# The query and key units of the first mixer take their accumulators from five PSUM banks in fixed pairs, instead of from a rotation of three and a side pair

## What is computed

```python
u = rmsnorm(x, g_mix)
q, k, v, z, xbc, dt, g_a, g_s = split(u @ w_in)      # weights of 2048 rows
q, k = apply_rope(q), apply_rope(k)                  # 16 query heads, 4 key heads of 64
attn = sliding_window_sink_attention(q, k, v, sinks)
y = ssd_chunked(silu(conv4(xbc)), dt, ...)           # gated by z, normed
h = x + (sigmoid(g_a) * (attn @ w_attn_br) + sigmoid(g_s) * (y @ w_ssd_br)) @ w_o
h = h + (silu(f @ w_gate) * (f @ w_up)) @ w_down     # f = rmsnorm(h)
h = h + sigmoid(rmsnorm(h) @ w_ple_gate) * (p @ w_ple_proj)
x = rmsnorm(h)                                       # and then the second block:
q, kv, gates, conv_in = split(rms_norm(x) @ w_in_2)  # attention, a 31-tap convolution,
...                                                  # an output projection and a gated FFN
```

## Time and profile before

| | us |
|---|---|
| median of 3 runs (2759.24 to 2760.5) | 2760.45 |
| the profiled execution, its own time | 2762.22 |
| its span | 2760.4 |
| TensorE busy | 2713.8 (98%) |
| VectorE busy | 1961.4 (71%) |
| ScalarE busy | 1416.7 (51%) |
| GpSimd busy | 101.0 (4%) |
| DMA engines, mean busy share of q1 (weights) | 56.7% |

### The profile page before, as it was taken

How to read it: one execution, slowest core, us unless ns; L and a number is a source line. 1 busy time by engine, 2 the same in 40 slices (tenths; PEclk the granted TensorE clock), 3 DMA queues, 4 the chain that set the end, 5 groups by cost and what they waited for, 6 DMA issues and landing times.

```text
span 2760.4 us, 41660 instructions
## 1 busy us (share of the span) xinstructions
PE 2713.8 (98%) x16606; PEld 2383.3 (86%) x16606; DVE 1961.4 (71%) x2940; ACT 1416.7 (51%) x2102; POOL 101.0 (4%) x189
## 2 busy tenths in 40 slices
PE   8999999999999999999999999999999999999998
PEld 7788888888888888888888899988888888888887
DVE  7568777757677776677666778876788775677765
ACT  6455555544455554455445551256655553455543
POOL 1320000000000000000000000000000000000000
PEclk9999999999999999999999999999999999999999
DMA  7466556555568888877656566863355556555554
GB/s 240 135 197 227 176 180 194 184 187 193 197 225 287 279 282 297 294 275 276 208 186 204 185 194 229 277 236 98 133 179 200 187 190 192 181 191 192 183 195 141
DMA packets 166610, 573.19 MB, mean 208 GB/s; under 512 B 19872, under 2 KB 26736, under 8 KB 165904
## 3 DMA queue, kind: packets, MB, share of 16 engines
q1 hardware_dynamic: 151216, 521.86, 56.7%
q0 software_dynamic: 15056, 48.65, 4.9%
q10 hardware_dynamic: 144, 0.01, 0.0%
HBM read 530.86 MB, written 38.90 MB: 206 GB/s over the span
## 4 chain that ended last, share of the span: by engine, by line
PE 90%; DVE 6%; ACT 2%; DMA 1%; issue 1%; POOL 0%; DVEq 0%; SPq 0%; ACTq 0%; POOLq 0%
PE PS L950 89%; DVE wl L1914 1%; DVE CC L1922 1%; DMA raw<-in_w_in 1%; ACT wh L1371 1%; PE PS L1286 0%; DVE SQA L1914 0%; DMA XC<-KTC 0%; DVE QT L1914 0%; DVE Z L1914 0%; DVE H L1914 0%; ACT SX1b L1371 0%; DVE TC L1922 0%; DVE RB L1973 0%; DVE CC L1914 0%
## 5 line engine op out<-in xcount | busy, mean ns | idle before, releaser
L1914 DVE TENSOR_TENSOR wl<-raw,wh 128x1024 fp32r<-128x1024 f32 (+3 forms) x892 | 1044.2, 1195 | 464.5 <-ACT wh L1371 462.6
L1371 ACT ACTIVATE wh<-raw 128x1024 fp32r<-128x1024 f32 (+3 forms) x892 | 898.0, 1031 | 522.1 <-PE PS L950 416.0
L950 PE MATMUL PS<-CHt,wh 128*128 128x512 f32 x2816 | 886.1, 396 | 1.9 <-DVE wl L1914 1.9
L950 PE MATMUL PS<-BIGt,wh 128*128 128x512 f32 (+1 forms) x2816 | 757.4, 357 | 2.9 <-DVE TA L1914 1.2
L950 PE MATMUL PS<-AHt,wh 128*128 128x512 f32 (+1 forms) x2080 | 636.9, 386 | 14.1 <-DVE wl L1914 11.1
L950 PEld LDWEIGHTS PS<-CHt,wl 128*128 128x128 f32 x2816 | 529.0, 188 | 124.8
L950 PE MATMUL PS<-CHt,wl 128*128 128x256 f32 x2816 | 553.5, 278 | 0.0
L950 PEld LDWEIGHTS PS<-BIGt,wl 128*128 128x128 f32 x2304 | 436.0, 189 | 79.1 <-issue 0.2
L950 PE MATMUL PS<-BIGt,wl 128*128 128x256 f32 x2304 | 498.9, 279 | 0.0
L950 PEld LDWEIGHTS PS<-BIGt,wh 128*128 128x128 f32 x2816 | 436.1, 191 | 7.7 <-issue 4.9
L950 PEld LDWEIGHTS PS<-AHt,wl 128*128 128x128 f32 x1952 | 368.7, 189 | 80.0 <-issue 0.7
(11 more groups left out here) (307 smaller groups left out, 1633.5 us busy)
## 6 DMA issues: line engine op xcount, KB each, us to landing
raw<-in_w_up SPq DMA_DIRECT2D x264, 512.0 KB, 4.8
raw<-in_w_in SPq DMA_DIRECT2D x200, 512.0 KB, 4.2
raw<-in_w_down SPq DMA_DIRECT2D x132, 512.0 KB, 4.3
raw<-in_w_gate SPq DMA_DIRECT2D x88, 512.0 KB, 5.5
raw<-in_w_down SPq DMA_DIRECT2D x56, 384.0 KB, 3.6
raw<-in_w_ssd_br SPq DMA_DIRECT2D x32, 512.0 KB, 4.4
raw<-in_w_o SPq DMA_DIRECT2D x32, 512.0 KB, 4.3
PKR<-in_w_in SPq DMA_DIRECT2D x32, 512.0 KB, 5.3
```

The costliest lines, as they stand in the source:

```text
L950: return e.matmul(o, l, r, start=start, stop=stop, skip_group_check=True)
L1371: return e.activation(o, x, f, **k)
L1914: return e.tensor_tensor(o, x, y, op)
```

## The change

The four query units and the key unit get fixed pairs: `ev_q` 0: 0, 1; `ev_q` 1: 3, 4; `ev_q` 2: 2, 0; `ev_q` 3: 1, 3; `ev_k`: 4, 2. All five are now set aside, that is, they no longer move the counter `gb`. `bank_free` is changed so that a query or key unit waits for the last holder of bank 3 or 4 like for any other bank, and the first later unit that takes bank 3 or 4 waits for the scan (`ssd_d`) as before. The number and order of sub-steps and of all steps in the plan stay as they are.

```diff
-            banks=(3, 4) if i == 1 else (0, 1, 2),
+            banks=((0, 1), (3, 4), (2, 0), (1, 3))[i],
...
-    add("w_in", 0, 16, 1024, "U1", "ev_k", 0, mode="turn", gens2=[stage("full_u1", 0, 4)], gens=[("rope_k", 0, [0, None, 1, 2, None])])
+    add("w_in", 0, 16, 1024, "U1", "ev_k", 0, mode="turn", banks=(4, 2), gens2=[stage("full_u1", 0, 4)], gens=[("rope_k", 0, [0, None, 1, 2, None])])
...
-        aside = u.banks == (3, 4)
+        aside = u.ev in ("ev_q", "ev_k")
...
-            if prev is None or units[prev].ev == "ev_q" and b in (3, 4):
-                if prev is not None or b in (3, 4) and units[n].ev != "ev_q":
-                    e.wait_ge(ssd_d.sem, ssd_d.at(3, "xd1"))
+            ahead = ("ev_q", "ev_k")
+            if b in (3, 4) and units[n].ev not in ahead and (prev is None or units[prev].ev in ahead):
+                e.wait_ge(ssd_d.sem, ssd_d.at(3, "xd1"))
+                return
+            if prev is None:
                 return
             emptied(prev)
```

## The result

The changed kernel takes 2771.82 us (median of 6 runs, 2769.33 to 2775.31), against 2760.97 for the kernel before (6 runs, 2759.24 to 2764.48). The ratio is 1.0039, with a 95% interval of 1.0029 to 1.0049: slower by 10.9 us. The forecast was 2765.1 with a range up to 2769.0, so the time lies above the range. The profiled execution is the longest of the six (own time 2775.31, span 2773.5).

A forecast was written before the change was run, and what follows sets the result against it. TensorE, busy for 98% of the span, was taken to bound the kernel. The terms -5.0 - 1.7 + 8.8 + 2.6 = +4.7 us, on a median of 2760.45, gave 2765.1 us, range 2760.5 to 2769.

The forecast's parts named there:

- Step 1, the waits of TensorE: Query and key units: `ev_v` starts without its 3.2 us wait, at full clock (2.96 us), and ends 6.6 us earlier.
- Step 1, the keys: First scores: `KDU` lands at 87.3, TensorE idles 1.6 us without loss of clock, and 5.0 us is gained.
- The second rival: First scores: keys come later, TensorE stands 2.5 us or more and the clock falls; 2768.5 us, chance 0.12.
- Step 2: At `ev_z` 4: the 1.74 us wait goes, since the new holder was joined a unit earlier; 1.7 us gained.
- Step 3: Second mixer's start: `ev_ca` 0 waits for `ev_pg` 7's bank, net 8.8 us lost, plus 2.6 us for the clock.
- Steps 4 and 5: Joints at `ev_q2` 0 and `ev_h` 24: nothing lost at the first, 0 to 0.1 us at the second.
- the queue behind `ev_ca` 0: Second mixer: splits queued on ScalarE behind that wait have enough cover; counted as nothing, up to 1 us.

The follow-up runs named there:

- `keep_count`: The changed kernel with its new pairs, but the counter `gb` still moved by 8 in the five units as before: 2761.37 us, ratio 1.0002.
- `mixer_order`: The changed kernel with the second mixer's rotation written (1, 2, 0) for (2, 0, 1): 2759.12 us, ratio 0.9993.
- `hold_both`: The changed kernel with load 29 held until `RO<-KT` has landed and load 30 until `KDU` has: 2765.08 us, ratio 1.0015.
- `both_fixes`: The changed kernel with the second mixer's rotation (1, 2, 0) and loads 29 and 30 both held: 2755.24 us, ratio 0.9979.
- `after_again`: The changed kernel itself, unaltered, timed and profiled a second time: 2770.65 us, ratio 1.0032.
- `first_only`: The changed kernel with the second mixer's rotation (1, 2, 0) and only load 29 held: 2754.9 us, ratio 0.9975.

## Why the prediction was wrong

- **Step 1, the waits of TensorE: right.** 0.80 us for the `wl` of the key unit (0.8 predicted), no wait and a full clock at `ev_v`, arrival at the scores at 85.85 (85.7). The 2.96 us for the clock at `ev_v` came from a single execution, though. In `keep_count` the wait there was 3.68 us and the low clock lasted only from 73.55 to 76.8, of which half, 1.6 us, is lost.
- **Step 1, the keys: the step that failed.** It said "weight loads that now start sooner share the DMA engines, for which I take 0.2". They cost 2.1 us on `RO<-KT` in the first profile (82.25 against 80.14 for the rotation behind it) and 1.0 to 1.3 us in the other three with early loads, and in the first profile 2.7 us more on `KDU`. And it said "I count no loss of clock here", from a case with 1.74 us of idle time. For the wait that it forecast this held: behind 1.37 and 1.42 us the clock stayed at 1.00. But the wait had become 2.55 to 6.14 us, and the clock fell behind each of them. The gain of step 1 came out at 1.95 - 1.7 = 0.25 us (`mixer_order`, less the 1.7 us of `ev_z` 4; 2.5 us either way by the interval of that run) instead of 5.0. The base of the sum was sound: with the loads held the scores began at 87.31 for 87.3, and steps 1 and 2 together gave -5.8 for -6.7.
- **The second rival is what happened**, and I had it at 0.12. It gave 2768.5 because the keys' delay was counted as 0.9 us and the clock as 2.4. The whole collision costs 3.9 us in `mixer_order`, and 5.0 to 6.8 between the changed kernel and `hold_both` (+10.85 and +9.05, less the +4.0 of `hold_both`).
- **Step 2: right.** The wait of 1.74 us at `ev_z` 4 is gone.
- **Step 3: right.** The wait was 10.63 us for 10 to 11. Behind it the low clock lasted from 1628.35 to about 1634.4, of which half is lost, 3.0 us, and in `hold_both` 4.2 us, that is 2.1; I had 2.6 lost (the middle of my bounds, 1.65 and 3.35, is 2.5). With the 1.23 us that `ev_cg` 0 no longer waits, 10.1 - 1.2 + 3.0 = 11.9, or 11.0 with the clock of `hold_both`. The sum had 11.4. The runs give 9.8 (`hold_both` less `both_fixes`) and 12.7 (changed kernel less `mixer_order`, 2771.82 - 2759.12; 11.0 with +9.05 and -1.95). The Trainium skill, "TensorE: Matmul & The Clock Gate", Part 1, says that the number of matmuls at the low clock differs from run to run; the traces agree that it varies: the low clock lasted 6.0 us in the first profile, 4.6 in `after_again` and 4.2 in `hold_both`, behind the same wait.
- **Steps 4 and 5, and the queue behind `ev_ca` 0: right.** No new wait shows at `ev_q2` 0 or `ev_h` 24, and splits did not starve.
- **The sum.** -0.25 - 1.7 + 11.4 = +9.45 us, for a measured +9.05 and +10.9. In the first profile alone it is +2.4 for the first mixer, -1.7 for `ev_z` 4, +10.8 from there to the convolution `XC`, and 1.6 of small waits: +13.1. The forecast was 6.7 us too low against 2771.82. Of that, 4.75 us are step 1 and 0.5 us is the median before, which came out at 2760.97 for 2760.45; the last 1.5 us are within the 2 us by which the changed kernel's own two medians differ.

What stays open: the order of issue (load 30 ahead of the last `KDU` or behind it) fits the 2.7 us in one profile and the 0.7 or less in the others, but no run set that order on purpose. The share of the landing time that belongs to each DMA engine can't be read from these views.

## What to carry over

A wait that is taken from the engine that sets the pace also frees its input buffers sooner, and the large loads that waited for them go out sooner: look up which small transfer, one that some engine will wait for, is in flight just then, and if one is, hold the load for it (here one wait on SyncE for load 29 gave 4 to 5 us). When a change shifts a rotation, only the joints between rotations can change, so list them and find for each who held the bank and when it is emptied; a joint that got worse is mended by turning the tuple of the later rotation (9.8 to 12.7 us here). Both mends together make the idea pay: 2754.9 to 2755.2 us, 5.8 to 6.7 below the kernel before.

## What the runs showed of the hardware

- **Small transfers beside large ones.** The longest `RO<-KT` went from 4.2 to 4.9 us up to 5.5 to 6.5 with a load of 512 KB issued just ahead of the last of them. The Trainium skill, "DMA: Bandwidth & Descriptors", Queues, rings and completion order, says that each DMA engine goes in turn round the queues that have work for it, packet by packet. The trace agrees that both queues share the engines: from 89 to 90 us in the first profile after the change, 54 packets of q0 (GpSimd's) and 55 of q1 (the loads') start. It also shows that the small transfers can stand behind a load for long: from 87.5 to 89.0 there are 68 packets of q1 and none of q0, and the last two `KDU` landed at 91.06 and 91.85, behind load 30 (90.94). The last `RO<-KT`, beside load 29, landed 0.2 to 1.7 us ahead of it in all four profiles. What decides between the two cases no run here shows.
- **The clock's fall is not settled by the length of the wait alone.** Behind waits of 1.37 and 1.42 us at the scores the granted clock stayed at 1.00, and so it had behind 1.74 us at `ev_z` 4 before. Behind 1.87 us it fell to 0.50, and only 1.5 us after the work had begun again; behind 2.55, 2.59 and 3.38 us it fell too. Elsewhere in the kernel it stayed at 1.00 behind longer waits: 2.19 us at 2038.4 in `both_fixes` and 2.42 us at 2052.4 in `after_again`. At the same place in `hold_both` it fell behind 2.04 us. How long it then stayed low differed: 3.4 us in `first_only`, 10.3 us in the first profile after the change, of which 3.9 us were idle.
